# Output projection and second normalisation of eight of nine tiles moved from the mLSTM loop into the first tile's expert mixing, with the memory laid out anew

## What is computed

```python
def trunk_layer(x, c, ...):
    sh1, sc1, g1, sh2, sc2, g2 = silu(c) @ ada_w + ada_b
    h = rmsnorm(x, norm1_w) * (1.0 + sc1) + sh1
    z = h @ w_in + b_in
    ya = rglru(...z...); yb = mlstm(...z...)          # scan over 128-row tiles
    x = x + g1 * (concatenate([ya, yb]) @ w_out)      # output projection
    h2 = rmsnorm(x, norm2_w) * (1.0 + sc2) + sh2      # second normalisation
    return x + g2 * peer(h2, peer_wq, k1, k2, u, v)

def peer(xb, ...):                                    # 128 rows, 8 heads
    q = rmsnorm over 256 of (xb @ wq)                 # per head
    v1, i1 = top_k(q1 @ k1.T, 16); v2, i2 = top_k(q2 @ k2.T, 16)
    sv, si = top_k(v1[:, None] + v2[None, :], 16)     # 16 experts per row and head
    act = gelu(u[expert] . xb)
    return sum over experts of softmax(sv) * act * v[expert]
```

## Time and profile before

| what | value |
|---|---|
| median of 3 executions | 3338.17 us (3338.04 to 3338.71) |
| profiled execution: time, span of its instructions | 3335.66 us, 3333.9 us |
| mean granted PE clock, share of full | 0.673 |
| busy share of the span | PE 70%, DVE 66%, ACT 59%, POOL 37% |
| bytes moved | 1190.87 MB, mean 357 GB/s |
| first gather, last gather begin | 589.6 us, 3300.5 us |

### The profile page before, as it was taken

One profiled execution on the slowest core, in us unless ns is written; L12 is line 12 of the kernel. 1 busy time (PEld: TensorE's weight loads), 2 busy tenths in 40 slices (PEclk: granted clock), 3 DMA queues, 4 the chain that ended last, 5 costly groups with the idle time before them and its releaser, 6 DMA issues.

```text
span 3333.9 us, 45431 instructions
## 1 busy us (share of the span) xinstructions
PE 2317.2 (70%) x15134; PEld 1125.2 (34%) x15134; DVE 2216.5 (66%) x5475; ACT 1958.6 (59%) x6308; POOL 1248.7 (37%) x1133
## 2 busy tenths in 40 slices
PE   7999999777667666666666666666666666665553
PEld 5665455433334222332322232223222322232110
DVE  5687265666677767666666676666666666676654
ACT  3332143576666666666666666666666666666655
POOL 0000110354444544444444444444444444444332
PEclk9999999766666666665566656655566556655555
DMA  7231133999999999999999999999999999999997
GB/s 282 86 112 66 33 117 123 355 398 419 419 400 373 410 419 401 420 419 420 401 420 419 419 398 419 420 420 397 420 420 420 395 420 420 420 402 420 420 421 326
DMA packets 177566, 1190.87 MB, mean 357 GB/s; under 512 B 21066, under 2 KB 31338, under 8 KB 37682
## 3 DMA queue, kind: packets, MB, share of 16 engines
q0 software_dynamic: 155808, 1118.53, 82.0%
q1 hardware_dynamic: 21524, 69.45, 6.1%
HBM read 1178.64 MB, written 9.25 MB: 356 GB/s over the span
## 4 chain that ended last, share of the span: by engine, by line
DMA 37%; PE 33%; ACT 16%; DVE 7%; issue 3%; POOL 3%; SPq 0%; DVEq 0%; POOLq 0%; ACTq 0%
DMA r_w<-in_peer_uv,gidx 21%; PE ps L937 9%; DMA r_qk<-in_peer_uv,gidx 8%; DMA r_yT<-in_peer_uv,gidx 8%; PE ps L732 6%; PE ps L1000 6%; PE ps L879 3%; PE ps L789 3%; ACT mixc L1344 3%; DVE r_w L1934 3%; ACT mixc L1343 2%; ACT r_yT L1348 2%; ACT L1343 2%; POOL r_w L636 2%; ACT mixc L1341 1%
## 5 line engine op out<-in xcount | busy, mean ns | idle before, releaser
L636 POOL DMA_INDIRECT r_w<-in_peer_uv,gidx x678 | 787.3, 1161 | 969.7 <-PE ps L1000 892.3
L1000 PE MATMUL ps<-r_w,r_yT 128*32 128x256 f32 x5424 | 647.5, 575 | 609.4 <-ACT r_yT L1348 609.2
L1340 ACT ACTIVATE mixc<-mixc 128x1 f32<-128x1 f32 x1056 | 209.5, 198 | 613.7 <-DVE r_w L1934 380.7
L1934 DVE SCALAR_TENSOR_TENSOR r_w<-r_w,r_vo 128x1024 f32<-128x1024 f32 x341 | 416.1, 1226 | 199.7 <-DMA r_w<-in_peer_uv,gidx 199.1
L1934 DVE SCALAR_TENSOR_TENSOR r_w<-r_w,r_yT 128x1024 f32<-128x1024 f32 x337 | 410.2, 1223 | 161.4 <-DMA r_w<-in_peer_uv,gidx 152.6
L1000 PEld LDWEIGHTS ps<-r_w,r_yT 128*32 128x32 f32 x5424 | 141.2, 135 | 1070.4 <-ACT r_yT L1348 979.9
L1344 ACT ACTIVATE mixc<-mixc 128x1 f32<-128x1 f32 x1056 | 408.4, 387 | 35.1
L1343 ACT ACTIVATE mixc<-mixc 128x1 f32<-128x1 f32 x1056 | 395.1, 374 | 0.9
L1000 PE MATMUL ps<-r_yT 128*32 128x256 f32 x1808 | 221.6, 584 | 218.6 <-ACT r_yT L1348 218.4
L636 POOL DMA_INDIRECT r_yT<-in_peer_uv,gidx x226 | 252.0, 1115 | 305.3 <-PE ps L1000 278.7
L1348 ACT ACTIVATE r_yT<-prm,mixc 128x32 f32<-128x32 f32 x1056 | 339.5, 322 | 34.2
(11 more groups left out here) (311 smaller groups left out, 3601.4 us busy)
## 6 DMA issues: line engine op xcount, KB each, us to landing
r_w<-in_ada_w SPq DMA_DIRECT2D x18, 1024.0 KB, 5.4
r_w<-in_peer_uv,gidx POOLq DMA_INDIRECT x678
r_w<-in_w_lin SPq DMA_DIRECT2D x16, 512.0 KB, 7.0
r_vo<-in_x_prompt SPq DMA_DIRECT2D x8, 512.0 KB, 7.5
r_qk<-in_ada_w SPq DMA_DIRECT2D x2, 2048.0 KB, 16.6
r_w<-in_w_out SPq DMA_DIRECT2D x2, 2048.0 KB, 8.2
r_w<-in_x_prompt SPq DMA_DIRECT2D x8, 512.0 KB, 3.6
x_dram<-r_w POOLq DMA_DIRECT2D x8, 512.0 KB, 3.6
```

The source lines that it names most:

```text
L636: pool.indirect_dma_start(ring[i], None, table, bass.IndirectOffsetOnAxis(gidx_t[:, t % 2, h, c:c + 1], 0)).then_inc(e_ld[i], 16)
L1000: mm = nc.tensor.matmul(ps[c * DEC:(c + 1) * DEC, q // 2, (q % 2) * QC:(q % 2 + 1) * QC], diag[:, s % 4, :], row[:, D + c * QC:D + (c + 1) ...
L1340: wch.mark(nc.scalar.activation(sq[:, i:i + 1], d, ACT.Square, scale=GELU_C ** 0.5 / TANH_K))
L1934: V.scalar_tensor_tensor(ring[i][:, 0:D], ring[i][:, 0:D], TANH_K, xrep[b % 2], ALU.mult, ALU.mult, accum_out=dots[:, i:i + 1]).then_inc(d ...
```

## The change

Tile numbers t now run in their natural order for the projection. Only tile 0 is projected and normalised inside the mLSTM loop, at i = 3 to 5; its first query, scores and route follow at i = 6, 7 and 8, so that the first gathers are issued during the last iteration. Tiles 1 to 8 are projected between the first tile's slots, by the table `PROJECT_AT`. The x rows, the residual and `h2` get other buffers, the ring has 6 places up to slot 92 and 8 from there on, and the query weights have eight buffers of which four are also used for other things, so that heads 0 to 3 are loaded a second time for tile 1 (4 MiB more). The x1 store moves from POOL to SP. The sample's broadcast rows g1, a2 and sh2 are loaded by SP only after `scaled(7)`.

```diff
-RING = 8
-PLACES = 11
+RING = 6
+PLACES = 8
+JOIN = 92
-FAST = (2, 3, 12, 13, 14, 15)
-ROUTE_AT = {2: 2, 3: 10, 4: 22, 5: 37, 6: 53, 7: 69, 8: 85, 9: 101, 10: 116, 11: 132,
+FAST = (1, 2, 3, 8, 9, 12, 13, 14, 15)
+ROUTE_AT = {1: -4, 2: 7, 3: 13, 4: 22, 5: 37, 6: 53, 7: 69, 8: 92, 9: 102, 10: 116, 11: 132,
+PROJECT_AT = {t: 4 + 10 * (t - 1) for t in range(1, NT)}
...
 # SP
+            def load_x(t):
+                if t >= 2:
+                    sp.wait_ge(x1_st[t % 2], 16 * (t // 2))
+                    sp.wait_ge(x1_sq, t - 1)
+                    sp.wait_ge(h2_ready, t - 1)
+                sp.dma_start(xr[t % 2][0:rows(t)], x_rows[t].rearrange("t (c n) -> t c n", c=2)).then_inc(xr_ld[t % 2], 16)
...
+            sp.wait_ge(h2_ready, NT - 1)
+            row = mod_dram[1, 2 * D:3 * D].partition_broadcast(P)
+            sp.dma_start(g1p, row.rearrange("p (c n) -> p c n", c=2)).then_inc(bc_ld, 16)
...
+            for h in range(4):
+                load_wq(1, h)
...
 # POOL
-                if uses[n] > 1 or i < RING:
+                if uses[n] > 1:
                     pool.wait_ge(v_free, RING + last_use[n] + 1)
+                elif i < 4:
+                    pool.wait_ge(i_mm, (5, 7, 9, 9)[i])
+                elif i < RING:
+                    pool.wait_ge(d_exp, NT)
                 else:
-                    pool.wait_ge(y_st, 64 * joins(i - RING)[0])
...
+                    pool.wait_ge(o_mm, 2 * NT)
...
 # PE, in the loop over the slots, behind mix(s)
+                for u, at in PROJECT_AT.items():
+                    if u == NT - 1 and s == at:
+                        project(u, 0)
+                    elif u < NT - 1 and s - at in (0, 1, 5, 6):
+                        project(u, (s - at) // 5, range(4 * ((s - at) % 5), 4 * ((s - at) % 5) + 4))
...
 # ACT, behind weight(s)
+                    if s == at + (9 if u < NT - 1 else 4):
+                        x1_norm(u)
+                        x1_root(u)
...
 # DVE
+            def projected(t, c):
+                r, bank, x = rows(t), project_bank(t, c), xr[t % 2]
+                if c == 0:
+                    if t == 0:
+                        dve.wait_ge(bcp_ld, 48)
+                    if t == NT - 1:
+                        dve.wait_ge(bc_ld, 48)
+                    dve.wait_ge(xr_ld[t % 2], 16 * (t // 2 + 1))
+                dve.wait_ge(o_mm, 2 * t + c + 1)
+                if t < NT - 1:
+                    V.tensor_tensor(ptmp, ps[:, bank, :], g1p[:, c], ALU.mult).then_inc(o_ev, 1)
...
+                dve.wait_ge(o_ev, 2 * t + c + 1)
+                last = V.tensor_tensor(x[0:r, c], x[0:r, c], ptmp[0:r], ALU.add)
...
                 dot(s)
+                for u, at in PROJECT_AT.items():
+                    if s == at + 3:
+                        projected(u, 0)
+                    if s == at + (8 if u < NT - 1 else 3):
+                        projected(u, 1)
+                    if s == at + (11 if u < NT - 1 else 6):
+                        scaled(u)
```

More of the change, by code:

```diff
@@ new lines, in _ @@
+            sp.dma_start(outs[5][0, 0].rearrange("h (k j) -> k h j", j=1), cst[:, 0, :, DK:DK + 1],
+                         allow_slow_non_contiguous=True).then_inc(state_st, 16)
+            sp.wait_ge(y_ready, NT)
+            load_wq(0, 2)
+            load_wq(0, 3)
+            for h in range(2):
+                sp.wait_ge(q_mm, h + 1)
+                load_wq(0, 4 + h)
+            store_x1(1)
+            load_x(3)
+            for h in range(2, 4):
+                sp.wait_ge(q_mm, h + 1)
+                load_wq(0, 4 + h)
@@ new lines, in x1_norm, with x1_root @@
+            def x1_norm(t):
+                r = rows(t)
+                act.wait_ge(x1_ready, t + 1)
+                nc.scalar.activation(junk[0:r], xr[t % 2][0:r], ACT.Square, accum_out=ssq2[0:r, t:t + 1]).then_inc(x1_sq, 1)
+            def x1_root(t):
+                r = rows(t)
+                act.wait_ge(x1_sq, t + 1)
+                nc.scalar.activation(ssq2[0:r, t:t + 1], ssq2[0:r, t:t + 1], ACT.Sqrt, scale=1.0 / D,
+                                     bias=epsc[0:r]).then_inc(x1_rt, 1)
@@ L1829, in _, with scaled @@
-            mixed_heads(NT - 1)
-            gated(NT - 1)
-            dve.wait_ge(d_exp, NT)
-            V.tensor_scalar(jmk, jm, 0.5 / TANH_K, None, ALU.mult)
+                dve.wait_ge(o_ev, 2 * t + c + 1)
+                last = V.tensor_tensor(x[0:r, c], x[0:r, c], ptmp[0:r], ALU.add)
+                if c == 0:
+                    link(last)
+                else:
+                    last.then_inc(x1_ready, 1)
+            def scaled(t):
+                r, x = rows(t), xr[t % 2]
+                dve.wait_ge(x1_rt, t + 1)
+                link(V.reciprocal(rstd2[0:r, t:t + 1], ssq2[0:r, t:t + 1]))
+                for c in range(2):
+                    last = V.scalar_tensor_tensor(h2h(t, c)[0:r], x[0:r, c], rstd2[0:r, t:t + 1], a2b[0:r, c * 512:(c + 1) * 512],
+                                                  ALU.mult, ALU.mult)
+                link(last)
+                for c in range(2):
+                    last = V.tensor_tensor(h2h(t, c)[0:r], h2h(t, c)[0:r], sh2b[0:r, c], ALU.add)
+                last.then_inc(h2_ready, 1)
@@ L1985, in route @@
                 experts()
-            scaled(NT - 3)
-            projected(NT - 2, 0)
-            route(0)
-            projected(NT - 2, 1)
-            residual(NT - 2)
-            projected(NT - 1, 0)
-            copy_places(0)
-            scaled(NT - 2)
-            gates(0)
-            projected(NT - 1, 1)
-            residual(NT - 1)
+            keys(0)
+            weights(0)
+            for i in range(NT):
+                if i + 1 < NT:
+                    keys(i + 1)
+                if i == NT - 1:
+                    route(0)
+                carry(i)
+                if i == NT - 1:
+                    copy_places(0)
+                if i >= 1:
+                    mixed_heads(i - 1)
+                if i < 2:
+                    evict_unit(14 + 2 * i)
+                if i + 1 < NT:
+                    weights(i + 1)
+                if i == NT - 1:
+                    gates(0)
+                if i >= 1:
+                    gated(i - 1)
+                if i < 2:
+                    evict_unit(15 + 2 * i)
+                if i < 3:
+                    gate_out(3 + 2 * i)
+                    gate_out(4 + 2 * i)
+                if i == 3:
+                    projected(0, 0)
+                if i == 4:
+                    projected(0, 1)
+                if i == 5:
+                    scaled(0)
+                if i == NT - 2:
+                    V.tensor_scalar(jmk, jm, 0.5 / TANH_K, None, ALU.mult)
+            mixed_heads(NT - 1)
+            gated(NT - 1)
             for s in range(N_SLOTS):
@@ L2001, in _ @@
                 dot(s)
-                if s == 1:
-                    scaled(NT - 1)
-                    route(1)
-                if s == 2:
-                    copy_places(1)
-                if s == 3:
-                    gates(1)
+                for u, at in PROJECT_AT.items():
+                    if s == at + 3:
[4 more added lines that the diff above has]
+                        scaled(u)
                 if t and j == 1:
```

584 lines of the change are left out of this document (257 added, 327 removed).

## The result

The changed kernel takes 3415.24 us (median of 4, 3413.67 to 3416.43) against 3338.11 for the kernel before on the same chip: ratio 1.0234, 95% interval 1.0221 to 1.0247, some 77 us slower. Forecast were 3380 us, in a range of 3350 to 3415. The profiled execution has a span of 3411.9 us, 78.0 more than before.

What follows compares the result with a forecast made beforehand. PE was taken to bound the kernel up to the gathers, the DMA from there on. Gather 84's delay 26.5, reload 10.1 and quick routes 7 sum to 43.6 on a span of 3333.9, 3377.5, stated as 3380 us; range 3350 to 3415.

Steps and rivals of the forecast that it cites:

- dot 74 to gather 84: End of first tile: dot 74 at 822.6, gather 84 issued at 849.4, with a 10 us stall between.
- The shorter loop: mLSTM loop without most projection: iterations 11.4 us instead of 18.7, first gather at 530 against 589.58, 59.5 earlier.
- the 12 us: mLSTM loop: at half clock heads and two turns add about 3 us an iteration, 12 in all; carried into the range.
- The first mix: Start of the first tile's slots: first mix at 551.3 instead of 607.92, 56.6 us earlier.
- The period: Ten slots per tile while tiles 1 to 7 are projected: 38 us each, on a chain through PE, DVE and ACT.
- The clock: PE in the periods: mean clock 0.85, costing pieces and mixes 2.9 us more a period.
- The broadcast rows: Behind the periods: DVE waits in projected(8, 0) for the sample's rows, a stall of 5 to 14 us, taken as 10.
- Gather 84: Behind the periods: issued at 849.4, lands like a lone MiB (6.1 us) at 856.4, against 829.9 before: +26.5 us.
- Reload and the quick routes: DMA-bound stream after gather 84: 4 MiB of query weights +10.1 us, routes 8 and 9 in FAST +7.
- Three places less: Gather ring in later tiles: 8 places read 419 to 420 GB/s as with 11, so the loss is priced at nothing.
- The pieces hide: Rival, periods: loop DMA-bound at 28.3 us a period, 3312 us; chance 0.25 together with periods of 29 to 31.5.
- Mostly half clock: Rival, periods: PE mostly at half clock, 42 to 47 us a period, 3408 to 3443 us; chance 0.12.

Runs made afterwards that it cites:

- e2: Changed kernel with one matmul instead of four in each of the 28 projection pieces, three quarters of the products left out: 3349.15 us, ratio 1.0035.
- e3: Changed kernel with DVE's add of each half projection behind the dots at + 5 and + 10 instead of + 3 and + 8, nothing left out: 3376.12 us.
- e9: Changed kernel with tile 0's queries of heads 2 to 7 using two of eight row blocks: 3406.59 us, ratio 1.0217.
- e10: Changed kernel with tile 0's replicates writing 128 of 512 columns from the fourth group on: 3402.98 us, ratio 1.0207.
- e8: Changed kernel with ten more matmuls on PE behind the mix one slot ahead of each half's first piece: 3444.78 us, ratio 1.0317.
- e1: Kernel before the change with 8 places instead of 11, so the ring never grows: 3339.81 us, ratio 1.0007.
- e7: Changed kernel with only a quarter of each query weight reloaded for tile 1, 3 of 4 MiB left out: 3404.86 us, ratio 1.0202.
- e6: e5 with the short pieces of e2, one matmul in place of four: 3333.03 us, ratio 0.9988.
- e5: e3 with DVE's gates of routes 1 to 7 one slot later and their copy_places two slots later, nothing left out: 3379.02 us, ratio 1.0118.

## Why the prediction was right in sign and wrong in size

The forecast said slower, by way of a chain through the pieces; it was 34 us short. Its own steps against the profile (span 78.0 more, 43.6 forecast) add up to that: the first mix +6.9, the periods +30.2, dot 74 to gather 84 -4.7, gather 84 to its dot +2.3, the same dot in the kernel before +2.6, dots 84 to 100 -1.3, the rest -1.7.

- **The shorter loop: right, partly by luck.** First gather at 531.3, forecast 530; first dot 56.1 earlier. Small misses cancel: iteration 3 began at 446.20, not 449.57, and took 20.8 us, not 18.7; from its end to route 0 it was 53.4, not 50.1; the route took 10.9 to the gather, not 11.6. PE's clock in the loop fell to 0.70 as the text allowed for, and cost little of the 12 us.
- **The first mix: 7 late.** It begins at 558.27, forecast 551.3. `query(0, 1)` stands on the chain ahead of the first weight, as the row below shows, and takes 6.12 us after an idle PE, where 3.73 was the row at full clock. Slot 4's dot starts at 563.5, not 556.6: +6.9.

```profile
548.67 6.12 PE L953 MATMUL ps<-r_qk,r_w 128*128 128x128 f32 x32
...
554.83 0.39 ACT L1310 ACTIVATE r_qk<-ps 128x256 f32<-128x256 f32 x1 [5.32 <-PE ps L953]
```

- **The period: 42.3, forecast 38. This is the step that failed**, "I take 38 us a period", with 7 x 4.3 = 30.2 of the 34 us. The mechanism is the one named: e2 (pieces short, 66 us back) and e3 (add later, 39 back) show it from two sides; the two overlap and don't add up. Mis-sized was what else stands on the chain. The chain of waits puts 120 us on the pieces, 17.2 a period, and 13.8 with 2.9 for the clock were forecast; but 29 on mixes, 20.5 on queries and 20.2 on replicates, that is 4.2, 2.9 and 2.9 a period, where 2.6, 0.4 and 0.7 were counted. The text took a query for hidden except one ("3 of a query"). With DVE's dots held up behind the piece there was nothing for it to hide behind; that reason is argued, and e9 gives back 0.8 us a period for two thirds of the queries. e9 and e10 show that these shares are not what their removal gives, so how the 4.3 divides stays open. (The "eight pieces" of the forecast's clock term are a slip: a period has four, and the 2.9 is worked out from their 13.8 us and four mixes.)
- **The clock: as sized, for the pieces.** Mean 0.81 in the periods, forecast 0.85; first pieces 5.0 us, second 3.7. Seven periods with two first pieces each lose 14 x 1.3 = 18 us on that, and 7 x 2.9 = 20 was forecast. The Trainium skill ("TensorE: Matmul & The Clock Gate", "What's actually happening") says that activity releases the throttle. e8 doesn't bear that out for the small matmuls added there: PE was busier, 88% against 79%, and the granted clock 0.79 against 0.81.
- **The broadcast rows: no stall.** SP issued them from 868.04 on, and `projected(8, 0)` began at 873.76 having waited 2.02 us for PE. In a queue that isn't full they land quickly, where the row before had 15.5 in a full one; the bound of 5 to 14 was too high at both ends. Other runs have a stall: DVE waited 4.9 us for these rows in e2, where the DMA had been at 0.95, and 2.8 in e10. Dot 74 to gather 84 is 22.1 us, not 26.8: -4.7. There is no stall of 10, but the rest of that stretch took 5.3 more than counted.

```profile
r_hT<-mod_dram SPq DMA_DIRECT2D x1, 512.0 KB, 3.7
```

The line of the DMA issues stands above, the timeline here:

```profile
868.04 0.38 SPq L546 DMA_DIRECT2D r_hT<-mod_dram  x1
...
873.76 0.84 DVE L1815 TENSOR_TENSOR r_qk<-ps,r_hT 32x256 f32<-32x256 f32 x2 [2.02 <-PE ps L907]
```

- **Gather 84.** It went out at 881.83 and its dot began at 891.15, 9.3 us later, where 7.0 was counted. In the kernel before its dot began at 827.3, not 829.9: the 17.7 us that the text took for its landing is a row of the last third, with 11 places, and e1 has 7.6 to 15.8 in the periods with 8.
- **Reload and the quick routes: right.** From dot 84 to dot 100 the kernel before takes 40.9 us and the changed one 56.7: 15.8, forecast 17.1. By e7 the reload is 8.1 x 4 / 3 = 10.8 of it, forecast 10.1; the remaining 5.0 fall to the routes 8 and 9, forecast 7. That division is by subtraction, the routes weren't tried alone.
- **Three places less: right**, by e1. The slices that the text read as having 8 places (15 to 19) lie mostly behind slot 284, which begins at 1351 us, in slice 17, where the ring has grown; the slices also go down to 373 GB/s, not 398.
- **The rivals.** "The pieces hide" fell: the period is 42.3 and the DMA at 0.79, and even e6, without three quarters of the pieces, needs 30.5 a period, not 28.3. "Mostly half clock" had the right period and time (42 to 47, 3408 to 3443) for the wrong reason, with the clock at 0.81. The limit between "faster" and "slower" was put at a period of 32 us; e2 with 32.9 is 0.35% slower, and e6 with 30.5 is level, 0.12% faster, so that held roughly.

## What to carry to other kernels

Work moved from a stage bound by one engine into a stage bound by the DMA costs time if an engine's queue makes the stage's own chain wait for it: DVE, which had to pick up the result two slots later, waited 6.9 us a half for 8.7 us of matmul, and dots, weights and gathers waited with it. Put the pick-up later where the buffers allow (here that alone gave back 39 of 77 us), and count on the chain everything that the same engine does between, at the clock it has after waiting. It isn't enough by itself: a second wait moved in the same way (e5) gave nothing. When the chain of waits shows shares, a share is not the gain of removing it: two lines of 20 us, cut by 68% and 52%, gave 6 and 7.

## What the runs showed of the hardware

- Ten fp32 matmuls of 128x64 a half, put into PE's pauses (e8), didn't raise its granted clock: 0.79 at 288.0 of 329.1 us busy, where the changed kernel had 0.81 at 234.0 of 296.2 and e3 0.85 at 228.3 of 262.5.
- The landing time of a 1 MiB gather goes with how many are in flight. Its median is 6.8 us in the periods of the changed kernel, and 11.2 in those of e1 with 8 places. Between 3000 and 3300 us it is 15.8 in e1 with 8 places and 23.2 in the kernel before with 11, and they move 419 and 420 GB/s. A 512 KB broadcast load landed in 3.7 us in the changed kernel, with few gathers in flight. A bound for a stall must be taken at the filling that the changed kernel will have there.
